# Second block of a two-block sequence model: a pair's two heads in one TensorE step, and seven background sequences that follow a written list

## The reference, cut to what matters

```python
def second_block(x, mem, ...):
    h = rms_norm(x, g[0]);  p = h @ w_in_first           # 2*512 conv columns, 1792 RWKV columns
    y_conv = conformer_conv(p[..., :1024], ...)          # gate, causal conv of width 31, layer norm, silu
    y_rwkv, _ = rwkv7_mix(p[..., 1024:], ...)            # 8 heads of 64
    y = concatenate([y_conv, y_rwkv], -1) @ w_out        # then cross-attention and swiglu

def rwkv7_recurrence(r, w, k, v, kk, a):                 # one head, one token
    s_kk = S @ kk_t
    S = S * w_t - outer(s_kk, kk_t * a_t) + outer(v_t, k_t)
    y_t = S @ r_t
```

## Time and profile before

| | |
|---|---|
| median of 3 runs | 1756.98 us (1756.47 to 1758.47) |
| the profiled execution, whole / its span | 1757.04 us / 1755.1 us |
| instructions in the span | 26846 |
| PE, DVE, ACT, POOL busy | 95%, 48%, 35%, 22% of the span |
| PE matmul records | 11510 |

### The profile page before, as it was taken

How to read it: one execution, slowest core, us unless ns; L and a number is a source line. 1 busy time by engine, 2 the same in 40 slices (tenths; PEclk the granted TensorE clock), 3 DMA queues, 4 the chain that set the end, 5 groups by cost and what they waited for, 6 DMA issues and landing times.

```text
span 1755.1 us, 26846 instructions
## 1 busy us (share of the span) xinstructions
PE 1661.0 (95%) x11510; PEld 1365.6 (78%) x11510; DVE 838.8 (48%) x1256; ACT 606.0 (35%) x973; POOL 389.4 (22%) x333
## 2 busy tenths in 40 slices
PE   6999999999999999999998877898999999999997
PEld 5789878787888888888776666777878878888876
DVE  3377642435433333344756887645642632333334
ACT  4143432324323232243335442334334432222222
POOL 2112111212201011133034540103102341131133
PEclk8899999999999999999999889999999999999999
DMA  5123421224222223222411100013211222223222
GB/s 195 61 84 121 145 73 49 76 87 150 97 96 94 98 76 108 80 96 84 144 50 49 49 3 3 3 50 108 109 41 56 97 88 105 75 94 103 89 78 66
DMA packets 29829, 146.03 MB, mean 83 GB/s; under 512 B 4096, under 2 KB 7440, under 8 KB 14608
## 3 DMA queue, kind: packets, MB, share of 16 engines
q1 hardware_dynamic: 29712, 144.33, 23.4%
HBM read 138.03 MB, written 6.29 MB: 82 GB/s over the span
## 4 chain that ended last, share of the span: by engine, by line
PE 77%; DVE 8%; issue 7%; POOL 4%; ACT 3%; DMA 1%; POOLq 0%; SPq 0%; DVEq 0%; ACTq 0%
PE ps L153 76%; POOL zf L165 3%; DVE zf L165 3%; DVE zf L173 2%; DVE wl L165 1%; DVE ps L173 1%; ACT zf L159 1%; ACT zf L162 1%; ACT wh L162 1%; DMA raw<-in_wstream 1%; ACT zr L162 1%; POOL tn L165 1%; PE ps L156 1%; DVE zf L2344 0%; DVE zr L173 0%
## 5 line engine op out<-in xcount | busy, mean ns | idle before, releaser
L153 PE MATMUL ps<-zr,wh 128*128 128x512 f32 (+1 forms) x3936 | 1173.7, 383 | 16.2 <-DVE wl L165 9.9
L153 PEld LDWEIGHTS ps<-zr,wh 128*128 128x128 f32 x3936 | 716.6, 190 | 175.2 <-DVE wl L165 9.8
L153 PE MATMUL ps<-zr,wl 128*128 128x512 f32 (+1 forms) x1968 | 745.7, 379 | 0.0
L165 POOL TENSOR_TENSOR zf<-zf 128x512 f32<-128x512 f32 (+1 forms) x237 | 283.5, 1203 | 856.4 <-ACT zf L159 587.5
L153 PEld LDWEIGHTS ps<-zr,wl 128*128 128x128 f32 x1968 | 374.0, 190 | 77.1 <-issue 0.8
L165 DVE TENSOR_TENSOR wl<-raw,wh 128x1024 fp32r<-128x1024 f32 (+1 forms) x243 | 306.2, 1300 | 230.5 <-ACT wh L162 230.3
L162 ACT ACTIVATE wh<-raw 128x1024 fp32r<-128x1024 f32 (+1 forms) x243 | 240.4, 1038 | 213.6 <-PE ps L153 211.8
L159 ACT ACTIVATE zf<-zf 128x512 f32<-128x512 f32 (+2 forms) x232 | 127.5, 561 | 396.3 <-DVE zf L165 282.2
L153 PE MATMUL ps<-zf 64*64 64x64 f32 (+6 forms) x3640 | 203.3, 248 | 32.3 <-DVE zf L165 18.1
L153 PEld LDWEIGHTS ps<-zf 64*64 64x64 f32 (+3 forms) x3640 | 162.7, 150 | 72.7 <-issue 31.1
L165 DVE TENSOR_TENSOR zf<-ps,zf 128x512 f32<-128x512 f32 (+2 forms) x165 | 97.6, 597 | 202.8 <-PE ps L153 176.0
(11 more groups left out here) (94 smaller groups left out, 713.1 us busy)
## 6 DMA issues: line engine op xcount, KB each, us to landing
raw<-in_wstream SPq DMA_DIRECT2D x117, 1024.0 KB, 4.8
zf<-in_xT SPq DMA_DIRECT2D x16, 256.0 KB, 3.1
raw<-in_wstream SPq DMA_DIRECT2D x4, 768.0 KB, 4.3
kv_scratch<-zf SPq DMA_DIRECT2D x8, 256.0 KB, 2.2
x_scratch<-zf SPq DMA_DIRECT2D x8, 256.0 KB, 2.1
zf<-x_scratch SPq DMA_DIRECT2D x8, 256.0 KB, 4.4
out<-zf SPq DMA_DIRECT2D x16, 128.0 KB, 1.7
zf<-in_cu SPq DMA_DIRECT2D x1, 1256.0 KB, 10.1
```

Of the source, the lines that this page charges most:

```text
L153: return self.raw.matmul(out_, l, x, start=start, stop=stop)
L165: return self.raw.tensor_tensor(out_, a, b, o)
```

## The change

1. **Two heads in one step.** The steps `a`, `pk`, `rt`, `qt`, `tz`, `x` and `z` take a pair of heads: 16 matmuls that alternate between the heads, into two banks. In `prod` each head's input already lies in its own half, so the four combinations of input and output half occur by turns. In `x` and `tz` the second head's result goes to the other half of the partitions, and `z` reads it from there. `ta`, `px` and `gh` keep their form and run for both heads in a row. Both heads' semaphore counts come at the end of the common step. On the other engines the same instructions stand, first for head 0 and then for head 1 (`both`).
2. **Two head generators in place of four**, pairs 0 and 2, and pairs 1 and 3.
3. **A written list.** `TURNS` is a string of 429 characters. Each letter advances one of seven generators (c conv on DVE, g conv on POOL, p prep, h and i heads, f fin, o `w_out`) to its next step; a dot ends the turns after one half of a dense tile. `step`'s round-robin, its paces and `lag` are not used in this stage. The generators have more stopping points, so that a turn is smaller.

```diff
-LAG = 1
+TURNS = """
+.....pppp..p.pp..ppp.pg.p.pgg.cccccpcg.phhgcc.cgcgghghg.ggchggc.chhcc.chcccc.hgg.chcgggh.ccg.hc.c.pc
...
+    def turns_to_stop(self):
+        if self.acts > self.seen:
+            for name in self.turns:
+                if name == ".":
+                    break
+                self.turn(name)
+            self.seen = self.acts
...
-    pl.begin(prep, bg_head(0, 0), bg_head(0, 1), bg_head(1, 0), bg_head(1, 1), bg_fin())
+    pl.follow(TURNS, c=bg_conv(), g=bg_conv_pool(), p=bg_prep(), h=bg_head(0), i=bg_head(1), f=bg_fin(), o=bg_out())
...
-    pl.begin(bg_out())
-    pl.drain()
+    pl.turns_to_end()
...
-            def prod(what, lhs, rhs, hp, hh):
-                K, s0 = ("head." + what, hp, hh), 64 * hh
-                e.wait_ge(freed(*K), *prep_done(hp))
+            def prod(what, lhs, rhs, hp):
+                K = "head." + what
+                for hh in range(2):
+                    e.wait_ge(freed(K, hp, hh), *prep_done(hp))
                 for _, rows_, cs, bl in CHUNKS:
-                    t = e.mm(ps(*K)[rows_, bl], lhs[s0:s0 + 64, cs], rhs[s0:s0 + 64, cs])
-                t.then_inc(*e.up("mm", *K))
+                    t = [e.mm(ps(K, hp, hh)[rows_, bl], lhs[hs, cs], rhs[hs, cs]) for hh, hs in enumerate(HALVES)]
+                    if bl.stop == 256 and rows_.stop == 128:
+                        done2(t, K, hp)
...
+            def head_x(hp, lv):
+                K = "head.x"
+                for hh in range(2):
+                    e.wait_ge(freed(K, hp, hh, lv), ("head.ta", hp, hh), ("head.z", hp, hh, lv - 1))
+                for a, rows_, _, bl in CHUNKS:
+                    h = rows_.start // 64
+                    t = [e.mm(ps(K, hp, hh, lv)[HALVES[h ^ hh], bl], head_bufs(hp, hh)[1][rows_, bl],
+                              head_bufs(hp, hh)[2][rows_, bl]) for hh in range(2)]
+                    if (a, h) == (3, 1):
+                        done2(t, K, hp, lv)
...
+            def head_z(hp, lv):
...
+                    t = [e.mm(ps(K, hp, hh, lv)[rows_, bl], head_bufs(hp, hh)[3][HALVES[h ^ hh], bl],
+                              head_bufs(hp, hh)[0][HALVES[h ^ hh], bl]) for hh in range(2)]
```

## The result

The changed kernel takes 1697.58 us (median of 4 runs, 1694.22 to 1700.54) against 1757.62 us beside it, a ratio of 0.9653 (0.9641 to 0.9664): 60 us less. Forecast were 27, in a range that ended at 1709. The direction was right, the size was not. The profiled execution took 1700.54 us, with a span of 1698.6.

A forecast was written before the change was run, and what follows sets the result against it. PE was taken to bound A and C, neither PE nor DVE B; after the change DVE bounds B. 115 + 118 + 83 = 316 against 343.3, 27 us less: 1730 us, 8-in-10 range 1709 to 1750.

The forecast's parts named there:

- B: Middle stretch, from the last `p` tile to the first `wa` matmul: 153.6 to 118 us, DVE becoming the bound.
- scaled by PE's work (74 / 90.6): In B: DVE's idle time falls from 30.5 to 25 us, in proportion to PE's work.
- A: First stretch, ending with the last `p` tile: 131.4 to 115 us, PE's work 107.2 and 8 idle.
- The 5.2 us stays: In A: PE's wait for ACT's square behind `prep.kk` remains, since kk and norm are still one half tile apart.
- the quarters' 35.7: Over all pairs: 76 common steps on four quarters save 0.47 us each, 35.7 us of PE.
- C: Last stretch, from `wa` to the end of `kt`: 58.3 to 83 us, mostly B's work moved.
- The common step: In the heads: 32 records cost 0.47 us where two single steps cost 0.94.
- the wait of 3.7 us: In A: PE's wait for ACT's copy of a transpose ahead of `head.a`, expected to go.
- `fin.s` rounds: In C: five rounds of the last pair leave PE idle some 0.4 us each, 2 us.
- DVE packs tightly: Rival in B: 102 us, DVE's 93 and 9 idle; 43 us less, 1714 us; chance 17%.
- The clock rival: In B: PE's granted clock falls to 0.75, 74 us become 85, B about 132; 1744 us; chance 13%.
- The slower case: In B: taps wait behind late evictions on DVE; at 60 us DVE idle 1765 us; chance 8%.

The follow-up runs named there:

- e2: The changed kernel's written list with single steps, head 0's 8 matmuls then head 1's, each in its own two quarters: 1713.53 us, 0.9736.
- e1: The changed kernel's common steps on four quarters, but the old round-robin order with its lag in place of the list: 1754.43 us, 0.9977.
- e11: The changed kernel, but in B x, tz, the transpose or product between and z of one level stand directly behind one another: 1716.42 us, 0.9766.
- e3: The changed kernel, but in x, tz and z both levels of a head keep the same output half, interleaved on two quarters: 1713.73 us, 0.9747.
- the second profile: From the unchanged changed kernel run again, beside the repeat of the version with seven list entries moved in B: 1699.41 us, 0.9663.

## Why the prediction was wrong

**The step that failed is what the list does to waiting.** The prediction said of B that DVE's idle time, "scaled by PE's work (74 / 90.6)", is 25 us, and of A: "The 5.2 us stays". Both take the old order's waits and carry them over. The list alone is worth 45 us and the quarters alone 4 (e2, e1); the forecast's 27 was made of the quarters' 35.7, less what B hides. It had the right cause for the smaller part. The windows divide the 58 us of the three stretches: 16 are the quarters inside the list (302.1 to 286.2), 42 the list (343.9 to 302.1). Taken the other way round the quarters are 5 and the list 53, so some 11 us need both. Of the list's 42, 26 lie in A (131.4 to 105.8) and 16 in B and C (212.5 to 196.3), into which some 4.5 us of A's work had moved besides. e11 shows by what order can do this: with nothing of other sequences between a step and its user B and C are 14 us longer than in the changed kernel's first profile and 18 longer than in its second, and DVE's waits for PE on L173 are as long as in the old order. It brings back 14 to 18 us, of the 24 that the list is worth in B and C. That the old order was slow for this reason is likely and not shown: prep in groups cost nothing, taps in sixes 6, and how one pair's end overlaps with the next pair's start was not tried by itself.

**The common step**: right. 0.47 us, and with two quarters 0.93 (e3). e2 and e3 show what it is worth inside the list: 16 us, from 25 us of PE's busy time.

**A**, 99.3 for 115. Idle 1.35 us, not 8: 6.6 us. PE 97.95, not 107.2: 9.3 us. More than half of these were low clock. The 120.2 us of the earlier trace rows holds two stretches at the 1.2 GHz level, the windows of the kernel before:

```profile
881.40:884.80 3.40, 3.40 (x9) 2.63 (x8) 3.30 (x6) 1.15 (x2) 1.55 (x1) 0.50 0.00 0
959.90:970.20 10.30, 7.08 (x20) 5.50 (x20) 4.65 (x7) 4.07 (x6) 4.26 (x3) 0.50 0.27 95
```

The first follows the wait of 3.7 us, which ended at 880.2; the second sets in during the wait of 5.2 us, which ended at 963.1. PE was busy for 10.5 us of them at about half its pace, an estimate of 5.2 us. Without the waits A's clock is 1.00. I took PE's busy time as work, and it wasn't. The rest, about 4 us, was gained ahead of A, as shown above.

**B**, 102.35 for 118. DVE 85.6 and not 93; idle 16.8 and not 25, half of the miss each. The first is a plain mis-sizing. By their shapes, the seven operations of v, scale and shift that left B took 8.4 us with them and not 4.8, for some had run beside POOL; the split isn't in B at all (2.4); and of conv and `cat` seven operations came, 4.6 us, not ten and 7. Smaller terms about offset one another. The second is the step above. The prediction's rival "DVE packs tightly" gave 102 for B, but from 93 of DVE's work and 9 of idle time, and the trace shows 85.6 and 16.8: its number is right partly by luck. With A as it came, it would have given 1698.

**C**, 84.6 for 83: right within 2 us, with its `fin.s` rounds at 2.0 us of waiting in five times, as forecast. Two small misses offset one another in it, 81.6 of busy time for 77.8 and 3.0 of idle time for 5.

**The clock rival** had a point: B's granted clock is 0.82 (0.86 in the second profile), and PE's work in B is 79 us busy for a forecast 74. But it takes back a few us, not 26: PE was idle for 23 us of B and not for 44. Where the waits stayed, in the old order, the clock of B fell from 0.88 to 0.80 with the shorter steps (e1).

**The slower case**, DVE behind a waiting instruction: DVE's longest wait for PE in B is 1.8 us. Not seen.

What was missing is a test of the list by its distances. The written orders of both kernels and the trace together would have allowed it: for each head step, what stands on PE and DVE between it and its user, before and after.

## What to carry to other kernels

Where two engines alternate and neither is full, time saved on one of them in the old order turns mostly into waiting and low clock: here some 32 us of PE work brought 4. Put other sequences' work between a step and its user first; then the same saving brought 16. And when a wait goes, look at the clock behind it: busy time at the lower level is not work that has to be done.

## What the runs showed of the hardware that was not expected

DVE operations with both inputs in SBUF take longer while POOL runs, those that read PSUM don't. DVE's timeline of the changed kernel, at pair 2's `head.a`, and then POOL's:

```profile
1018.89 0.41 DVE L173 TENSOR_TENSOR zf<-ps,cu_sb 128x256 f32<-128x256 f32 x1
1019.34 2.44 DVE L173 TENSOR_TENSOR zf<-zf,cu_sb 128x256 f32<-128x256 f32 x2
```

```profile
1017.42 4.08 POOL L173 TENSOR_TENSOR zf<-zf 128x512 f32<-128x512 f32 x3 [3.96 <-ACT zf L170]
```

Without POOL two of these take 0.89 us (at 974.00). The Trainium skill (SBUF — State Buffer, "SBUF: two separate sides") says that an operation of DVE with two SBUF inputs and one of GpSimd that reads SBUF exclude each other; the trace agrees in that 0.9 us become 2.4 under three POOL additions. Summed over DVE's operations in B whose inputs are both in SBUF and that overlap with one of POOL, each against the shortest of its kind, it is 7.8 us before and 8.0 after, so it is no part of the gain, but it makes the longest wait left in B (4.5 us, `tz` of level 4).
